# Attention scores' low-key products as two 64-row matmuls, and group copies and query splits moved between VectorE, ScalarE and GpSimd, in a one-core encoder layer

## The chip, the cores and the metric

The kernel runs on one core of one Trainium2 chip. The metric is the device time of one execution in microseconds (us), lower is better. Before the change it was 1474.98 us, the median of three runs (1473.99 to 1475.79).

## The reference

One encoder layer over two sequences, a prompt of 512 tokens and a sample of 1024, with d_model 1024. A normalised input is projected by one matrix to 8 query heads, 2 key heads and 2 value heads of width 64, and to 512 pooling columns. Queries and keys are normalised per head and rotated by position. The part that the change touches is the attention (bidirectional, four query heads for each key head):

```python
s = jnp.einsum('bqkgd,bskd->bkgqs', qi, k, preferred_element_type=jnp.float32) * scale
p = jax.nn.softmax(s, axis=-1).astype(v.dtype)
return jnp.einsum('bkgqs,bskd->bqkgd', p, v)
```

The pooling group, an output projection with residual, and a squared-ReLU MLP (4096 wide) follow. All inputs are float32.

## The kernel before, in words

Float32 operands are split into a rounded high part (type F32R) and a low remainder, and products are summed in PSUM. In the projections and the MLP three products are made of each pair (`three`, L943 to L945: high by high, and the two cross products). The stages are: projection of 12 tiles of 128 tokens, attention of the prompt, attention of the sample, output projection, MLP up and MLP down.

**Attention.** A job is one head's 512 queries against 512 keys for two heads at once (prompt: 4 jobs, called pairs, each with two halves) or one head's 512 queries against 1024 keys (sample: 4 pairs of 4 jobs, `idx` 0 to 3). Each job has 8 steps `k` and 4 score groups `u`. In each step TensorE turns one key tile's probabilities (`transpose_p`, four 128-column transposes, L1088) and multiplies another's with the values (`values`, high and low, L1103 and L1104). In every odd step it also makes the scores of one group of a job that is one or two ahead (`scores`, L1070 and L1072). A group is two 512-column PSUM banks.

**The stacked operands of the scores.** A head is 64 wide and the array has 128 rows. `Qs` holds the high part of the queries on one half of the 128 partitions and the low part on the other. `KA` holds the keys' high part on both halves, `KB` the low part on both. So L1070 makes (q high + q low) by k high and L1072 makes (q high + q low) by k low, each as one matmul of 128 rows by 512 columns for each of the two banks: four in a group.

**Who does what.** ScalarE (ACT) writes `pThi` (rounded, from PSUM), the exponentials `prob` (L1424), the output `o_full`, and the prompt queries' high parts. VectorE (DVE) writes `pTlo` (L1837, PSUM minus `pThi`), the row maxima `nmax` (L1899), reciprocals (L1909), the prompt queries' low parts, and `group_values` (L2022), which gathers half of one key head's values from `V` into `Vg`, twice for each pair of the sample. GpSimd (POOL) makes the sample queries' high and low parts (`split_q`, L2516 and L2519), adds and scales the outputs (L2537, L2543), and computes the pooling windows of the sample (`window_step`). Engines run their own instruction streams in order, written out by hand, and meet at semaphores: a group's scores wait for the exponentials of the group two before (two sets of banks), the `values` matmul waits for `pTlo`, `pTlo` waits for `pThi`, and `pThi` for the transposes. The SP queue moves the other half of each output by DMA (`move_out`) and spreads the reciprocals.

**The end of the projection.** In the last block, VectorE rotates tile 10 (`rotate`, which waits in the middle for a product from GpSimd), and then makes the low values of tile 11 (`split_v`, L1913) and its sum of squares (L1920). TensorE's second score group waits for that `split_v`, since it writes the bank from which it reads. In the same stretch VectorE makes the low queries of pair 1 of the prompt.

Of the kernel before, what the change touches and what calls it, by code (L numbers as in the profile page):

```python
# [7 lines left out]
ALU = mybir.AluOpType  # L8
# [5 lines left out]
P = 128  # L14
# [37 lines left out]
def hybrid_layer(nc, x, g1, w_in, gqk, w_pool, pool_scale, w_out, g2, w_up, w_down,  # L52
                 ident_d, rope_d, edge_d, y):
    with ExitStack() as ctx:
# [3 lines left out]
        def at(name, off, shape, dt=F32):  # L58
            return nc.alloc_sbuf_tensor_at(name, [P] + shape, dt, offset=BASE + off)
# [62 lines left out]
        o_full = at("o_full", S, [2, 512])  # L122
        o_part = at("o_part", S + 4096, [512])
        rinvb = at("rinvb", S + 32768, [512])
        rinvb_last = at("rinvb_last", R + 38912, [512])
        rinvd = nc.dram_tensor("rinvd", [3 * NQ, P, 4], F32).ap()
        sw_sample = [at(f"sw_sample{i}", S + 22528 + i * 4160, [SEQ_S + 2 * PAD]) for i in range(2)]
# [808 lines left out]
        def _(pe):  # L936
# [115 lines left out]
            def scores(s, pair, idx, u):  # L1052
                g = s.group(pair, idx, u)
                half = u // 2 if s.n == 0 else 0
                if u % (GRP // s.halves) == 0:
                    pe.wait_ge(q_lo[s.n], s.out(pair, idx, half) - NQ * s.n + 1)
                pe.wait_ge(k_dup[0], 32 + 32 * s.n)
                if s.n == 0:
                    pe.wait_ge(k_dup[1], 32)

                if not isinstance(g, int) or g >= 2:
                    pe.wait_ge(exp_done, g - 1)
                kv = pair_kv(pair)
                for h in range(2):

                    qt = u if s.n else 2 * (u % 2) + h
                    key0 = h * 512 * s.n
                    out = ps[:, 2 * (u % 2) + h]
                    q = Qs[:, 2 * s.parity(pair, idx) + half, qt * P:(qt + 1) * P]
                    pe.matmul(out, q, KA[s.n][:, bass.ds(kv, 1), key0:key0 + 512].rearrange("p a c -> p (a c)"),  # L1070
                              start=True, stop=False)
                    mm = pe.matmul(out, q, KB[s.n][:, bass.ds(kv, 1), key0:key0 + 512].rearrange("p a c -> p (a c)"),  # L1072
                                   start=False, stop=True)
                mm.then_inc(s_done, 1)

# [107 lines left out]
            scores(seqs[0], 1, 0, 2)  # L1183
            for pair in range(NQ // 2):
                attend(seqs[0], pair)
            with pe.Fori(0, NQ // 2 - 1) as pair:
                attend(seqs[1], pair)
            attend(seqs[1], NQ // 2 - 1, True)

# [142 lines left out]
        def _(act):  # L1332
# [66 lines left out]
            def split_q(s, pair, idx, unit):  # L1399

                j = s.job(pair, idx)
                act.wait_ge(qT_in[s.n], 16 * s.len // P)
                half = s.half_of(idx, unit * s.kts)
                a, c0 = half * 64, s.start + idx // 2 * 512

                if not isinstance(j, int) or j >= 2:
                    act.wait_ge(s_done, GRP * (j - 1))
                if isinstance(j, int) and j == 0 and unit == 0:

                    act.wait_ge(hT_lo, TT)  # L1410
                copy(blocks(Qs[a:a + 64, 2 * s.parity(pair, idx) + unit]), qk_cols(a, pair, c0, 512)).then_inc(q_hi, 1)

            def exps(s, pair, idx, u):
# [79 lines left out]
            def copy_out(s, pair, idx, half):  # L1493
# [5 lines left out]
                    act.wait_ge(o_saved, 2 * n - 3)  # L1499
                copy(o_full[:, half], ps[:, 7]).then_inc(o_copied, 1)  # L1500

            def split_wp():
                act.wait_ge(wp_scaled, 1)
                copy(wphi[:], wpT[:]).then_inc(wp_hi, 1)
# [16 lines left out]
            def attend(s, pair, last=False):  # L1521
                for idx in range(s.per):
                    for k in range(STEPS):
                        if last and (idx, k) == (2, 3):
                            exps(*exped_in(s, pair, idx, k))
                        if last and (idx, k) == (2, 5):
                            split_wp()
                        if transposed_in(s, pair, idx, k):
                            split_p(*transposed_in(s, pair, idx, k))
                        if k % s.kts == s.kts - 1:  # L1530
                            copy_out(s, pair, idx, s.half_of(idx, k))
                        if s.n == 0 and pair == 1 and k == 1:
                            split_q(s, 3, 0, 1)
                        if exped_in(s, pair, idx, k) and not (last and (idx, k) == (2, 3)):
                            exps(*exped_in(s, pair, idx, k))
                        if s.n == 0 and pair == 0 and k == 5:
                            split_q(s, 3, 0, 0)
                        if s.n == 0 and pair == 0 and k == 4:
                            split_q(s, 2, 0, 1)
                        if last and (idx, k) == (2, 6):  # L1540
                            split_c(0)
                        if last and (idx, k) in ((3, 0), (3, 2), (3, 4), (3, 6)):
                            split_folded(k // 2)
# [286 lines left out]
        def _(dve):  # L1830
# [99 lines left out]
                dve.wait_ge(qn_done, FIRST + t + 1)  # L1930
                dve.tensor_tensor(qn[:], qn[:], gqkb[:], ALU.mult).then_inc(qg_done, 1)

            def rotate(t, i):
                dve.wait_ge(qg_done, t + 1)
                dve.wait_ge(rope_in[i % 2], 16 * (t // 2) + 16)

                dve.wait_ge(rT_done, t)
                r = roped[:]
                dve.tensor_tensor(r, qn[:], rope[:, i % 2, 0].unsqueeze(1).to_broadcast([P, NQK, HEAD]),
                                  ALU.mult).then_inc(cos_done, 1)  # L1940
                dve.wait_ge(cos_done, FIRST + t + 1)
                dve.wait_ge(sin_done, FIRST + t + 1)
                dve.tensor_tensor(r, r, qsin[:], ALU.add).then_inc(rope_done, 1)
                dve.wait_ge(rope_done, FIRST + t + 1)
                if t >= 2:
                    dve.wait_ge(rT_out, 64 * (t - 1))
                dve.transpose(rT[t % 2][:], r.rearrange("p (j h) (q c) -> p h q j c", h=2, q=2).rearrange("p h q j c -> p (h q) j c")).then_inc(rT_done, 1)
# [36 lines left out]
            def project_block(n, last):  # L1984
                for i in range(2 if n == 0 else 0, 4):
                    t = n * 4 + i
                    split_v(t, qkv_banks(i) + 1)
                    sum_squares(t)
                    if t + 2 < TT:
                        split_hT(t + 2, (i + 2) % 4)  # L1990
                    if t + 3 < TT:
# [1 line left out]
                    if last and i == 1:  # L1993
# [2 lines left out]
                        split_k(0, 1)  # L1996
                        split_q(0, 0)
                        split_q(0, 1)
                    if last and i == 2:
                        split_q(1, 0)  # L2000
                        split_q(1, 1)
                    if last and i == 3:
                        maxes(seqs[0], 0, 0, 0)
                    scale_qk(t)
                    gain_qk(t)
                    if last and i == 3:
                        maxes(seqs[0], 0, 0, 1)
                    rotate(t, i)
                    if i % 2 and not (last and i == 3):
                        save_u_columns(t // 2)  # L2010

# [1 line left out]
            for n in range(NB - 1):  # L2013
                project_block(n, False)
            project_block(NB - 1, True)

            def group_values(pair, part):

                k0, k1 = part * 4, part * 4 + 4  # L2020
                t0 = SEQS[1][0] // P
                dve.tensor_copy(Vg[:, k0:k1], V[:, t0 + k0:t0 + k1, bass.ds(pair_kv(pair), 1), :]  # L2022
                                .rearrange("p t a d -> p t (a d)").bitcast(F32)).then_inc(vg_done, 1)

            def split_p(s, pair, idx, k):
                dve.wait_ge(pT_hi, s.turn(pair, idx, k) + 1)
# [27 lines left out]
            def attend(s, pair, last=False):  # L2054
                for idx in range(s.per):
                    for k in range(STEPS):
                        if s.n == 0 and pair == 2 and k == 2:
                            group_values(0, 0)
                        if last and (idx, k) == (2, 3):
                            scale_wp()  # L2060
                        if s.n and idx == 3 and k == 6 and not last:

                            dve.wait_ge(pv_done, s.turn(pair, 3, 4))
                            group_values(pair + 1, 0)
                        if transposed_in(s, pair, idx, k):
                            split_p(*transposed_in(s, pair, idx, k))
                        if s.n and (idx, k) == (0, 2):

                            dve.wait_ge(pv_done, s.turn(pair, 0, 0))
                            group_values(pair, 1)  # L2070
                        if inverted_in(s, pair, idx, k):
                            inverses(*inverted_in(s, pair, idx, k))
                        if scored_in(s, pair, idx, k):
# [338 lines left out]
        def _(pool):  # L2412
# [93 lines left out]
            def split_q(s, pair, idx):  # L2506
# [4 lines left out]
                if done:  # L2511
                    pool.wait_ge(win_step, done)
                pool.wait_ge(qT_in[s.n], 16 * s.len // P)
                pool.wait_ge(s_done, GRP * (s.job(pair, idx) - 1))
                pool.wait_ge(q_hi, NQ + m - 1)
                pool.tensor_scalar(blocks(Qs[a:a + 64, 2 * (idx % 2)]), qk_cols(a, pair, c0, 512), 1.0, 1.0, ALU.mult, ALU.mult  # L2516
                                   ).then_inc(q_hi, 1)
                pool.wait_ge(q_hi, NQ + m)
# [43 lines left out]
            def split_k(kv, low, part=0):  # L2562
# [9 lines left out]
                else:  # L2572
# [3 lines left out]
                                       blocks(KA[1][a:a + 64, kv, c].bitcast(F32)), ALU.subtract).then_inc(k_lo, 1)  # L2576
                    pool.wait_ge(k_lo, NKV + kv + part + 1)

            pool.wait_ge(u_saved, FIRST + TT // 2)

            pool.wait_ge(u_done, FIRST + TT // 2)
            window_step(done)
            done += 1
            pool.wait_ge(win_step, done)
            pool.wait_ge(q_hi, 5)
            pool.wait_ge(q_lo[0], 4)
            pool.tensor_tensor(blocks(Qs[64:, 0]), qk_cols(0, 2, 0, SEQ_P), blocks(Qs[0:64, 0].bitcast(F32)), ALU.subtract).then_inc(q_lo[0], 1)
            pool.wait_ge(q_lo[0], 5)
            for s in seqs:
                for pair in range(NQ // 2):  # L2590
                    for idx in range(s.per):
# [163 lines left out]
```

## Time and profile before

| | |
|---|---|
| median of three runs | 1474.98 us |
| the profiled execution's own time | 1475.89 us |
| its span | 1474.1 us |
| TensorE busy | 1463.4 us, 99% of the span |
| VectorE, ScalarE, GpSimd busy | 72%, 49%, 27% |
| mean granted TensorE clock | 0.999 of full speed |

Busy time of TensorE is modelled: the record of a 512-column matmul is about 0.39 us long, and the next one starts 0.23 us after it. What a matmul costs in a stream is therefore read from the starts, not from the length of a record. For the other engines too the records overlap a little at their ends. "Idle before" is the time in which an engine stood still ahead of a record, with the one that released it.

### The profile page before, as it was taken

How to read it: one execution, taken by the hardware profiler on the slowest of the kernel's cores; microseconds unless marked ns; L12 is line 12 of the kernel's file. 1: busy time of each engine (PE TensorE's matmuls, PEld its weight loads, DVE VectorE, ACT ScalarE, POOL GpSimd, SP SyncE). 2: the span in 40 equal slices, each digit the busy share in tenths (PEclk: the TensorE clock that was granted, in tenths of full speed). 3: DMA queues.
4: the chain of work that ended last, by engine and by line, in shares of the span. 5: the costliest groups of instructions: out<-in, count | busy, mean ns of one | idle time of the engine just before them, and what ended most of it. 6: DMA issues, size and time to landing. Idle time of an engine off the chain costs nothing.

```text
span 1474.1 us, 23234 instructions
## 1 busy us (share of the span) xinstructions
PE 1463.4 (99%) x7812; PEld 1306.9 (89%) x7812; DVE 1055.7 (72%) x1254; ACT 729.1 (49%) x1251; POOL 398.1 (27%) x363
## 2 busy tenths in 40 slices
PE   9999999999999999999999999999999999999999
PEld 8999878888888889999999999999888888888887
DVE  6765799999868785544454454449887888878875
ACT  6232398888847755545555554546322322323220
POOL 3457567666745420000000000001220211311300
PEclk9999999999999999999999999999999999999999
DMA  8644341111245849333233334347644344343434
GB/s 263 149 119 118 82 126 34 40 25 24 81 164 192 292 154 380 128 144 141 103 143 133 136 114 151 121 174 278 253 157 158 100 157 126 117 155 109 138 97 183
DMA packets 94443, 212.30 MB, mean 144 GB/s; under 512 B 12080, under 2 KB 31408, under 8 KB 94256
## 3 DMA queue, kind: packets, MB, share of 16 engines
q1 hardware_dynamic: 92192, 200.46, 40.8%
q10 hardware_dynamic: 2192, 11.08, 1.8%
q8 instruction: 33, 0.54, 0.2%
q14 instruction: 26, 0.21, 0.1%
HBM read 133.08 MB, written 71.62 MB: 139 GB/s over the span
## 4 chain that ended last, share of the span: by engine, by line
PE 97%; ACT 1%; DVE 1%; issue 1%; DMA 0%; POOL 0%; ACTq 0%; SPq 0%; DVEq 0%; POOLq 0%
PE ps L943 24%; PE ps L944 24%; PE ps L945 24%; PE ps L1206 6%; PE ps L1088 4%; PE ps L1216 3%; PE ps L1103 2%; PE ps L1070 2%; PE ps L1104 2%; PE ps L1072 2%; ACT prob L1424 0%; DMA ident<-in_ident 0%; ACT pThi L1339 0%; PE ps L968 0%; PE ps L972 0%
## 5 line engine op out<-in xcount | busy, mean ns | idle before, releaser
L943 PE MATMUL ps<-h,wuhi 128*128 128x384 f32 (+1 forms) x904 | 301.5, 333 | 0.2 <-issue 0.2
L944 PE MATMUL ps<-h,wuhi 128*128 128x384 f32 (+1 forms) x904 | 301.1, 333 | 0.0
L945 PE MATMUL ps<-h,wulo 128*128 128x384 f32 (+1 forms) x904 | 301.1, 333 | 0.0
L943 PE MATMUL ps<-wdhi,hidhi 128*128 128x512 f32 x672 | 261.6, 389 | 0.0
L945 PE MATMUL ps<-wdhi,hidlo 128*128 128x512 f32 x672 | 261.5, 389 | 0.0
L944 PE MATMUL ps<-wdlo,hidhi 128*128 128x512 f32 x672 | 261.5, 389 | 0.0
L2328 DVE TENSOR_TENSOR yacc<-yacc,ps 128x1024 f32<-128x1024 f32 x167 | 203.1, 1216 | 78.8 <-PE ps L945 78.8
L1339 ACT ACTIVATE hidhi<-hin 128x1024 fp32r<-128x1024 f32 (+1 forms) x72 | 86.8, 1205 | 301.0 <-PE ps L945 291.8
L2242 DVE TENSOR_TENSOR u<-u,ps 128x384 f32<-128x384 f32 x96 | 53.0, 553 | 181.6 <-PE ps L945 181.6
L943 PEld LDWEIGHTS ps<-h,wuhi 128*128 128x128 f32 x904 | 169.7, 188 | 0.7 <-issue 0.4
L944 PEld LDWEIGHTS ps<-h,wuhi 128*128 128x128 f32 x904 | 169.7, 188 | 0.0
L945 PEld LDWEIGHTS ps<-h,wulo 128*128 128x128 f32 x904 | 169.7, 188 | 0.0
L943 PEld LDWEIGHTS ps<-wdhi,hidhi 128*128 128x128 f32 x672 | 126.1, 188 | 26.8 <-issue 0.4
L944 PEld LDWEIGHTS ps<-wdlo,hidhi 128*128 128x128 f32 x672 | 126.1, 188 | 26.1
L945 PEld LDWEIGHTS ps<-wdhi,hidlo 128*128 128x128 f32 x672 | 126.1, 188 | 26.1
L2684 POOL TENSOR_TENSOR hout<-h,hout 128x384 f32<-128x384 f32 x1 | 1.7, 1748 | 477.3 <-PE ps L945 477.3
L1837 DVE TENSOR_TENSOR pTlo<-ps,pThi 128x512 fp32r<-128x512 f32 x160 | 107.9, 686 | 12.4 <-ACT pThi L1339 9.6
L1837 DVE TENSOR_TENSOR hidlo<-hin,hidhi 128x1024 fp32r<-128x1024 f32 (+1 forms) x72 | 111.5, 1549 | 5.4 <-ACT hidhi L1339 5.4
L1643 ACT ACTIVATE hout<-u 128x384 f32<-128x384 f32 x96 | 50.4, 525 | 124.8 <-DVE u L2242 113.5
L1339 ACT ACTIVATE pThi<-ps 128x512 fp32r<-128x512 f32 x160 | 95.0, 601 | 26.4 <-PE ps L1088 19.7
L1088 PEld LDWEIGHTS ps<-ident,prob 128*128 128x128 f32 x640 | 79.3, 140 | 22.7 <-DVE pTlo L1837 1.4
L1424 ACT ACTIVATE prob<-ps,nmax 128x1024 f32<-128x1024 f32 (+1 forms) x96 | 93.0, 974 | 11.5 <-DVE nmax L1899 11.3
(229 smaller groups left out, 2813.8 us busy)
## 6 DMA issues: line engine op xcount, KB each, us to landing
hd<-hout SPq DMA_DIRECT2D x64, 384.0 KB, 3.2
hin<-hd SPq DMA_DIRECT2D x48, 512.0 KB, 3.6
hd<-hout SPq DMA_DIRECT2D x32, 576.0 KB, 2.8
hin<-hd SPq DMA_DIRECT2D x24, 768.0 KB, 4.4
wuraw<-in_w_up SPq DMA_DIRECT2D x17, 1024.0 KB, 5.9
wdraw<-in_w_down SPq DMA_DIRECT2D x8, 2048.0 KB, 9.3
h<-h2d ACTq DMA_DIRECT2D x7, 1536.0 KB, 10.8
x2in<-in_x SPq DMA_DIRECT2D x12, 512.0 KB, 3.3
```

The lines of the kernel that those rows point to most:

```text
L943: pe.matmul(out, w_hi, m_hi, start=start, stop=False, skip_group_check=resumed)
L944: pe.matmul(out, w_hi, m_lo, start=False, stop=False, skip_group_check=resumed)
L945: return pe.matmul(out, w_lo, m_hi, start=False, stop=stop, skip_group_check=resumed)
L1088: mm = pe.transpose(ps[:, 4 + k % 3, qt * P:(qt + 1) * P], prob[s.parity(pair, idx)][:, u, c0:c0 + P], ident[:])
L1206: pe.matmul(ps[:, 2 * i + h], c[i][:, k], wohi[:, j, h * 512:(h + 1) * 512], start=(j == 0 and c is chi), stop=False)
L1216: mm = pe.matmul(ps[:, 2 * i + h], chi[i][:, SLOT_ROWS[j]], wolo[:, j, h * 512:(h + 1) * 512], start=False, stop=(n == KT - 1))
L1339: return act.activation(out, in_, ACT.Copy, **kw)
L1424: ins = act.activation(prob[b][:, u, c0:c0 + s.len], psw[:, (u % 2) * 1024 + c0:(u % 2) * 1024 + c0 + s.len], ACT.Exp, bias=nmax[:, b, q:q ...
L1643: act.activation(out, src, ACT.Relu).then_inc(relu_done, 1)
L1837: return dve.tensor_tensor(out, a, b.bitcast(F32), ALU.subtract)
L2242: dve.tensor_tensor(u, u, up_bank(par, (1, 4, 5)[k]), ALU.add).then_inc(u_sum, 1)
L2328: dve.tensor_tensor(q, q, down_banks(u, o), ALU.add).then_inc(acc_done, 1)
```

## The change

1. **Scores.** In `scores`, the two L1070 products come first, then the two with `KB`. For the prompt's pairs 0 and 1 these keep all 128 rows. For the prompt's pairs 2 and 3 and all of the sample each uses 64 rows: bank 0 is made from partitions 0 to 63 and bank 1 from 64 to 127, both with the high queries. (The product of the two low parts is left out there.) A new tile `Qh` holds the high queries on the half where `Qs` has the low ones. TensorE's loop over the sample's first three pairs is written out.
2. **Filling Qh.** ScalarE copies it for prompt pairs 2 and 3 (four copies of 64x512, behind a wait for the last pooling projection), GpSimd for the sample (one for each job).
3. **`group_values`** goes from VectorE to ScalarE, at the same steps.
4. **Low queries of prompt pair 1** go from VectorE's tile 10 to GpSimd, behind its product for tile 11's rotation.
5. **Tile 11's `split_v` and sum of squares** go into the middle of `rotate` of tile 10.

```diff
+        Qh = at("Qh", S + 34816, [2, 512], F32R)
...
                 for h in range(2):
-
-                    qt = u if s.n else 2 * (u % 2) + h
-                    key0 = h * 512 * s.n
-                    out = ps[:, 2 * (u % 2) + h]
-                    q = Qs[:, 2 * s.parity(pair, idx) + half, qt * P:(qt + 1) * P]
-                    pe.matmul(out, q, KA[s.n][:, bass.ds(kv, 1), key0:key0 + 512].rearrange("p a c -> p (a c)"),
+                    c, keys, out = part(h)
+                    pe.matmul(out, Qs[:, 2 * slot + half, c], KA[s.n][:, bass.ds(kv, 1), keys].rearrange("p a c -> p (a c)"),
                               start=True, stop=False)
-                    mm = pe.matmul(out, q, KB[s.n][:, bass.ds(kv, 1), key0:key0 + 512].rearrange("p a c -> p (a c)"),
+                for h in range(2):
+                    c, keys, out = part(h)
+                    if s.n == 0 and pair < 2:
+                        r = slice(0, P)
+                    else:
+                        r = slice(h * 64, h * 64 + 64)
+                    q = Qh[r, slot, c] if r.stop - r.start == 64 and h != high else Qs[r, 2 * slot + half, c]
+                    mm = pe.matmul(out, q, KB[s.n][r, bass.ds(kv, 1), keys].rearrange("p a c -> p (a c)"),
                                    start=False, stop=True)
...
-            with pe.Fori(0, NQ // 2 - 1) as pair:
+            for pair in range(NQ // 2 - 1):
...
+                if s.n == 0 and pair >= 2:
+                    act.wait_ge(u_done, FIRST + TT // 2)
+                    copy(blocks(Qh[64 - a:128 - a, s.parity(pair, idx)]), qk_cols(a, pair, c0, 512))
...
+            def group_values(pair, part):
+
+                k0, k1 = part * 4, part * 4 + 4
+                t0 = SEQS[1][0] // P
+                copy(Vg[:, k0:k1], V[:, t0 + k0:t0 + k1, bass.ds(pair_kv(pair), 1), :]
+                     .rearrange("p t a d -> p t (a d)").bitcast(F32)).then_inc(vg_done, 1)
...
+                        if s.n == 0 and pair == 2 and k == 2:
+                            act.wait_ge(v_lo, FIRST + TT)
+                            group_values(0, 0)
+                        if s.n and idx == 3 and k == 6 and not last:
+
+                            act.wait_ge(pv_done, s.turn(pair, 3, 4))
+                            group_values(pair + 1, 0)
+                        if s.n and (idx, k) == (0, 2):
+
+                            act.wait_ge(pv_done, s.turn(pair, 0, 0))
+                            group_values(pair, 1)
...
+                between()
                 dve.wait_ge(cos_done, FIRST + t + 1)
...
-                    if last and i == 2:
-                        split_q(1, 0)
-                        split_q(1, 1)
...
+                    if last and i == 2:
+                        def last_values():
+                            split_v(t + 1, qkv_banks(i + 1) + 1)
+                            sum_squares(t + 1)
+                        rotate(t, i, last_values)
...
+                pool.tensor_scalar(blocks(Qh[b:b + 64, idx % 2]), qk_cols(a, pair, c0, 512), 1.0, 1.0, ALU.mult, ALU.mult)
                 pool.tensor_scalar(blocks(Qs[a:a + 64, 2 * (idx % 2)]), qk_cols(a, pair, c0, 512), 1.0, 1.0, ALU.mult, ALU.mult
...
+            def split_prompt_q(pair, unit):
+
+                a, b, m = unit * 64, (1 - unit) * 64, 2 * pair + unit
+                slot = 2 * (pair % 2) + unit
+                pool.wait_ge(q_hi, m + 1)
+                pool.wait_ge(q_lo[0], m)
+                pool.tensor_tensor(blocks(Qs[b:b + 64, slot]), qk_cols(a, pair, 0, SEQ_P),
+                                   blocks(Qs[a:a + 64, slot].bitcast(F32)), ALU.subtract).then_inc(q_lo[0], 1)
+                pool.wait_ge(q_lo[0], m + 1)
+
+            pool.wait_ge(sin_done, FIRST + TT)
+            split_prompt_q(1, 0)
+            split_prompt_q(1, 1)
...
-            pool.wait_ge(q_hi, 5)
-            pool.wait_ge(q_lo[0], 4)
-            pool.tensor_tensor(blocks(Qs[64:, 0]), qk_cols(0, 2, 0, SEQ_P), blocks(Qs[0:64, 0].bitcast(F32)), ALU.subtract).then_inc(q_lo[0], 1)
-            pool.wait_ge(q_lo[0], 5)
+            split_prompt_q(2, 0)
```

## Rows read from the trace of the kernel before

**Rows 1.** The page: TensorE's busy time, and the ending chain by engine.

```profile
PE 1463.4 (99%) x7812; PEld 1306.9 (89%) x7812; DVE 1055.7 (72%) x1254; ACT 729.1 (49%) x1251; POOL 398.1 (27%) x363
...
PE 97%; ACT 1%; DVE 1%; issue 1%; DMA 0%; POOL 0%; ACTq 0%; SPq 0%; DVEq 0%; POOLq 0%
```

**Rows 2.** Stretches of the attention: busy time of each engine in each.

```profile
core 0: us, PE busy (x) PEld busy (x) DVE busy (x) ACT busy (x) POOL busy (x), PEclk, DMA share, GB/s
257.00:267.92 10.92, 10.92 (x66) 9.16 (x65) 10.16 (x14) 9.61 (x18) 7.83 (x9) 1.00 0.33 72
...
190.00:215.00 25.00, 24.05 (x133) 18.81 (x133) 23.37 (x33) 23.73 (x59) 15.99 (x14) 1.00 0.41 118
...
240.00:360.00 120.00, 120.00 (x707) 100.74 (x705) 113.24 (x149) 105.58 (x188) 81.09 (x65) 1.00 0.13 29
```

**Rows 3.** TensorE's timeline around one score group: start, length, line.

```profile
262.23 0.40 PE L1072 MATMUL ps<-KB,Qs 128*128 x1
262.47 0.39 PE L1070 MATMUL ps<-KA,Qs 128*128 x1
262.70 0.40 PE L1072 MATMUL ps<-KB,Qs 128*128 x1
262.93 0.39 PE L1103 MATMUL ps<-pThi,Vg 128*128 128x512 f32 x1
```

**Rows 4.** The weight loads of the same stretch.

```profile
261.89 0.19 PEld L1070 LDWEIGHTS ps<-KA,Qs 128*128 128x128 f32 x1
262.00 0.19 PEld L1072 LDWEIGHTS ps<-KB,Qs 128*128 128x128 f32 x1
262.24 0.19 PEld L1070 LDWEIGHTS ps<-KA,Qs 128*128 128x128 f32 x1
```

**Rows 5.** VectorE's groups in four sample jobs, 257 to 300.68 us.

```profile
L1837 DVE TENSOR_TENSOR pTlo<-ps,pThi 128x512 fp32r<-128x512 f32 x33 | 22.3, 687 | 2.1 <-ACT pThi L1339 1.4
L1899 DVE TENSOR_REDUCE nmax<-ps 128x1 f32<-128x1024 f32 x16 | 19.4, 1215 | 0.3
L2022 DVE CAST Vg<-V 128x512 fp32r x2 | 1.4, 694 | 0.0
```

**Rows 6.** ScalarE's and GpSimd's groups in the same four jobs.

```profile
L1339 ACT ACTIVATE pThi<-ps 128x512 fp32r<-128x512 f32 x33 | 19.7, 598 | 5.5 <-PE ps L1088 3.9
...
L2519 POOL TENSOR_TENSOR Qs<-QT,Qs 64x512 fp32r<-64x512 f32 x4 | 5.1, 1283 | 0.3
L2516 POOL TENSOR_SCALAR Qs<-QT 64x512 fp32r<-64x512 f32 x4 | 2.5, 629 | 0.4
```

**Rows 7.** The end of the projection, in order of time.

```profile
169.07 0.74 ACT L1442 ACTIVATE qksq<-qk 128x640 f32<-128x640 f32 x1
...
171.15 0.83 DVE L1943 TENSOR_TENSOR roped<-roped,qsin 128x640 f32<-128x640 f32 x1 [1.67 <-POOL qsin L2485]
...
172.78 0.31 DVE L1913 SCALAR_TENSOR_TENSOR V<-ps,rs,V 128x128 fp32r<-128x128 f32 x1
...
173.19 0.47 PE L1070 MATMUL ps<-KA,Qs 128*128 128x512 f32 x1 [1.31 <-issue]
```

**Rows 8.** The copy of values at 365 us and who works beside it.

```profile
365.10 2.39 POOL L2468 TENSOR_TENSOR up<-sw_sample,up 128x1024 f32<-128x1024 f32 x1
...
365.46 2.32 DVE L2022 CAST Vg<-V 128x512 fp32r x1
...
368.52 0.47 PE L1103 MATMUL ps<-pThi,Vg 128*128 128x512 f32 x1 [0.92 <-DVE pTlo L1837]
```

**Rows 9.** ScalarE's prompt outputs (one each half job) and a query copy.

```profile
194.61 0.59 ACT L1339 ACTIVATE o_full<-ps 128x512 f32<-128x512 f32 x1
...
213.19 0.59 ACT L1339 ACTIVATE o_full<-ps 128x512 f32<-128x512 f32 x1
...
235.42 0.59 ACT L1339 ACTIVATE o_full<-ps 128x512 f32<-128x512 f32 x1
...
185.88 0.63 ACT L1339 ACTIVATE Qs<-QT 64x512 fp32r<-64x512 f32 x1
187.34 0.69 ACT L1424 ACTIVATE prob<-ps,nmax 128x512 f32<-128x512 f32 x1 [0.83 <-DVE nmax L1899]
```

More of the change, by code:

```diff
@@ L1063, in scores, with part @@
                 kv = pair_kv(pair)
-                for h in range(2):
-                    qt = u if s.n else 2 * (u % 2) + h
-                    key0 = h * 512 * s.n
-                    out = ps[:, 2 * (u % 2) + h]
-                    q = Qs[:, 2 * s.parity(pair, idx) + half, qt * P:(qt + 1) * P]
-                    pe.matmul(out, q, KA[s.n][:, bass.ds(kv, 1), key0:key0 + 512].rearrange("p a c -> p (a c)"),
-                              start=True, stop=False)
-                    mm = pe.matmul(out, q, KB[s.n][:, bass.ds(kv, 1), key0:key0 + 512].rearrange("p a c -> p (a c)"),
+                slot = s.parity(pair, idx)
+                high = idx % 2 if s.n else half
+                def part(h):
+                    qt = u if s.n else 2 * (u % 2) + h
+                    return slice(qt * P, (qt + 1) * P), slice(h * 512 * s.n, h * 512 * s.n + 512), ps[:, 2 * (u % 2) + h]
+                for h in range(2):
+                    c, keys, out = part(h)
+                    pe.matmul(out, Qs[:, 2 * slot + half, c], KA[s.n][:, bass.ds(kv, 1), keys].rearrange("p a c -> p (a c)"),
+                              start=True, stop=False)
+                for h in range(2):
[6 more added lines that the diff above has]
+                    mm = pe.matmul(out, q, KB[s.n][r, bass.ds(kv, 1), keys].rearrange("p a c -> p (a c)"),
                                    start=False, stop=True)
@@ L1931, in gain_qk, with rotate @@
                 dve.tensor_tensor(qn[:], qn[:], gqkb[:], ALU.mult).then_inc(qg_done, 1)
-            def rotate(t, i):
+            def rotate(t, i, between=lambda: None):
                 dve.wait_ge(qg_done, t + 1)
@@ L1986, in project_block @@
                     t = n * 4 + i
-                    split_v(t, qkv_banks(i) + 1)
-                    sum_squares(t)
+                    if not (last and i == 3):
+                        split_v(t, qkv_banks(i) + 1)
+                        sum_squares(t)
                     if t + 2 < TT:
@@ L2007, in project_block @@
                         maxes(seqs[0], 0, 0, 1)
-                    rotate(t, i)
+                    if last and i == 2:
[3 more added lines that the diff above has]
+                        rotate(t, i, last_values)
+                    else:
+                        rotate(t, i)
                     if i % 2 and not (last and i == 3):
@@ L2015, in _ @@
             project_block(NB - 1, True)
[L2017 to L2023, printed above, removed]
             def split_p(s, pair, idx, k):
@@ L2056, in attend @@
                     for k in range(STEPS):
-                        if s.n == 0 and pair == 2 and k == 2:
-                            group_values(0, 0)
                         if last and (idx, k) == (2, 3):
                             scale_wp()
-                        if s.n and idx == 3 and k == 6 and not last:
-                            dve.wait_ge(pv_done, s.turn(pair, 3, 4))
-                            group_values(pair + 1, 0)
                         if transposed_in(s, pair, idx, k):
                             split_p(*transposed_in(s, pair, idx, k))
-                        if s.n and (idx, k) == (0, 2):
-                            dve.wait_ge(pv_done, s.turn(pair, 0, 0))
-                            group_values(pair, 1)
                         if inverted_in(s, pair, idx, k):
```

## The prediction

> **What bounds the kernel now.** I read the page first, then the stretches of the attention, then the timelines inside it. TensorE is busy 99% of the span and makes 97% of the chain that ended last [rows 1]: time leaves this kernel where TensorE gets shorter or waits less, provided that no neighbour takes over. Inside the sample's attention it never stands still: 120.00 of 120 us, and one job takes 10.92 us, while VectorE has 10.16 and ScalarE 9.61 us of records in it [rows 2]. So the neighbours are close behind, and how close decides what a shorter TensorE is worth. The prompt's attention differs: in 25 us TensorE has 24.05, ScalarE 23.73 and VectorE 23.37 us [rows 2], and a half job there took (213.19 - 194.61) / 3 = 6.19 us at first and (235.42 - 213.19) / 4 = 5.56 us later [rows 9], against the 10.92 / 2 = 5.46 us that TensorE's own work takes. There ScalarE sets the pace.
>
> **The score products.** Matmuls of 512 columns start 0.23 us apart [rows 3], so a group's four cost 0.93 us. If the two 64-row products run at the same time, the group has three such slots and saves 0.23 us. Prompt pairs 2 and 3 have 8 groups and the sample 64. Scores are made ahead: job 0 of the prompt makes three of them, each later job four, so 15 are made during the prompt and 57 during the sample, in 57 / 4 = 14.25 jobs. At full worth these 57 give 57 x 0.23 = 13.1 us.
>
> Do the neighbours follow? TensorE's job would be 10.92 - 4 x 0.23 = 10.0 us. VectorE, in four jobs of 43.68 us, stood idle 2.1 + 0.3 us and spent 1.4 us in the copies that now leave it [rows 5]: (43.68 - 2.4 - 1.4) / 4 = 9.97 us of a job. ScalarE stood idle 5.5 us [rows 6] and takes over the two copies, at about 0.6 us each like its own 128x512 copy `pThi` (598 ns): (43.68 - 5.5 + 1.2) / 4 = 9.85 us. Three engines within 0.15 us of one another, in fixed orders with handoffs between them, will not reach the longest of the three. I add 0.15 us a job: 10.15 us. The saving is 14.25 x (10.92 - 10.15) = **11.0 us**.
>
> What the trace of before cannot show is two matmuls side by side, since it has none. The bounds come from the nearest rows. Below: they start together, 0.23 us saved. 
>
> The Trainium skill speaks against this change on that point: "TensorEngine Tiling (Array Packing)", section Tiling Modes, Key Properties, says that changing the tiling mode, not just the tile, drains TensorE. No row of this kernel shows such a change. By that rule the case "above" would hold. The same skill's "TensorE: Matmul & The Clock Gate", Part 3, gives packed tiles a start some 4 ns apart; by that figure alone the 57 groups would give an estimated 57 x 0.226 = 12.9 us.
>
> **Filling Qh.** In the sample GpSimd gets one more copy for each job, 0.63 us [rows 6], on top of 7.83 us in 10.92 [rows 2]. The low queries queued behind it are due only in the next job's fourth step, so it costs nothing; if that cover were gone it would be 0.7 us a job. In the prompt ScalarE gets four copies at 0.63 us [rows 9]. The first stands before the exponentials of pair 1, where ScalarE waited 0.83 us for a maximum [rows 9]; that covers it. The other three fall between 195 and 213 us, where ScalarE sets the pace: **+1.8 us** with what is queued behind them, at the least 0. That the first copy now waits for the last pooling projection costs nothing, since the exponentials just ahead of it ended later than that.
>
> **The rest of the prompt.** From 213.19 us on, two jobs took 22.23 us. With TensorE at 10.0, the exponentials of 1024 columns taking over from pairs of 512, and one `group_values` (0.6) on ScalarE in the first of them, I put these at 10.75 and 10.1 us: **-1.4 us**.
>
> **The values of tile 11.** TensorE stood still 1.31 us before its second score group, which needs the `split_v` that VectorE began at 172.78 and ended 0.1 us before that group's start [rows 7]. VectorE itself had waited 1.67 us for GpSimd inside `rotate`, and ScalarE had finished `qksq` at 169.81 [rows 7]. Both moved operations (0.31 and 0.8 us) fit into that wait, so the whole idle time goes: **-1.3 us**. Next late would be the third group, which needs the first exponentials; these move up too, by some 0.9 us, since the two operations no longer stand before their maxima. The sum of squares also starts GpSimd's chain for tile 11 earlier, by some 2.5 us, which makes room there for the two low-query splits of pair 1 (1.28 us each, as L2519 [rows 6]) before the next group of scores. They cost nothing; if GpSimd were late, up to 2.6 us.
>
> **The copy at 365 us.** VectorE's `group_values` usually takes 0.69 us [rows 5], but this one took 2.32, ending with GpSimd's 2.39-us subtraction beside it, and TensorE then stood still 0.92 us [rows 8]. ScalarE does it now: **-0.9 us**. The other copies were hidden.
>
> Writing out TensorE's loop moves nothing that I can price: the loop's ends showed no idle TensorE [rows 2]. Taking the splits of pair 1 away from VectorE only fills a wait for GpSimd.
>
> **The sum.** -11.0 + 1.8 - 1.4 - 1.3 - 0.9 = -12.8 us. The profiled execution took 1475.9 us (span 1474.1 and 1.8 around it), so one like it would take 1463.1; the median was 0.9 below it, so **1462.2 us** is the forecast.
>
> **Rivals.**
> - *The loads take turns.* The second half product starts 0.11 us after the first. 57 x 0.12 = 6.8 us in place of 11.0, TensorE again alone as the bound: 1466.4 us. For it: loads never start closer than 0.11 us. Against it: they start well ahead of need.
> - *A neighbour becomes the bound.* Handoffs cost 0.5 us a job, not 0.15: the job is 10.5 us, saving 14.25 x 0.42 = 6 us: 1467.2 us. For it: VectorE's 9.97 us is as long as TensorE's.
> - *Nothing runs side by side.* The half products take a slot each. Then only -1.3, -0.9, -0.3 and +1.8 remain: about 1474.3 us.
> - *Slower: the array runs empty at each change of rows.* 72 groups x (0.32 - 0.23) = +6.5 us, with -0.7 from the other edits: about 1480.8 us. It decides against the change as soon as a change of rows costs over (0.23 + 0.01) / 2 = 0.12 us.
>
> **How the numbers follow.** Forecast 0.45, loads in turn 0.17, neighbour 0.14, nothing side by side 0.09, running empty 0.15. About 0.2% (3 us) is what a measurement of this kernel can tell from no change. The first three are faster, and part of the cases between: 0.77; within 0.2%: 0.09; slower: 0.14. The range starts where all 57 groups give 13.1 us and the prompt's copies hide (-16.7 us against the profiled execution, 1458.3) and reaches to the case of nothing side by side, 1474.5. The likeliest case's own range is 1459 to 1465.
>
> **What would show it.** In the changed trace the two `KB` products start within some 0.02 us, and the next matmul 0.23 us later; a sample job takes 10.0 to 10.3 us, with TensorE waiting now and then for `pTlo` or `prob`; the idle 1.31 and 0.92 us are gone; the prompt's first half jobs are longer than 6.19 us. The forecast is wrong if the second `KB` product, or the matmul after it, starts later than that, or if VectorE shows no idle time while TensorE does.

## The result: slower, and the profile after

The changed kernel takes 1484.55 us (median of six runs, 1483.89 to 1485.83) against 1474.8 for the kernel before (median of its six): a ratio of 1.0070, with a 95% interval of 1.0060 to 1.0081. That is 9.75 us slower where 12.8 us faster was forecast. The profiled execution took 1484.44 us with a span of 1482.6.

The page of the profile says first where the time is. TensorE is still the bound, and its busy time grew by 9.6 us over that of [rows 1], although it has the same number of instructions:

```profile
PE 1473.0 (99%) x7812; PEld 1286.2 (87%) x7812; DVE 1054.7 (71%) x1244; ACT 734.7 (50%) x1263; POOL 409.3 (28%) x381
...
PE 96%; ACT 1%; DVE 1%; issue 1%; DMA 0%; POOL 0%; ACTq 0%; SPq 0%; DVEq 0%; POOLq 0%
```

The stretch inside the sample's attention, as in [rows 2]. The second row is one job, now 11.58 us long instead of 10.92:

```profile
core 0: us, PE busy (x) PEld busy (x) DVE busy (x) ACT busy (x) POOL busy (x), PEclk, DMA share, GB/s
240.00:360.00 120.00, 120.00 (x669) 84.00 (x667) 106.24 (x137) 101.59 (x182) 83.60 (x74) 1.00 0.14 28
...
270.75:282.33 11.58, 11.58 (x67) 8.13 (x66) 10.18 (x14) 9.94 (x19) 7.77 (x7) 1.00 0.13 23
```

TensorE never waits there, and in 120 us it starts 669 matmuls where it started 707. VectorE is busy 106.24 us and not 113.24: it has become idler, so it is not the bound. What TensorE does with its time is seen in its timeline around a group (start, length, line; L1099 are the transposes, L1074 the products with `KA`, L1083 those with `KB`, L1114 and L1115 the values), to be read against [rows 3]:

```profile
243.33 0.60 PE L1099 MATMUL ps<-ident,prob 128*128 128x128 f32 x4
243.69 0.71 PE L1074 MATMUL ps<-KA,Qs 128*128 128x512 f32 x2
244.33 0.49 PE L1083 MATMUL ps<-KB,Qs 64*128 64x512 f32 x1
244.33 0.49 PE L1083 MATMUL ps<-KB,Qh 64*128 64x512 f32 x1
244.75 0.50 PE L1114 MATMUL ps<-pThi,Vg 128*128 128x512 f32 x1
245.09 0.39 PE L1115 MATMUL ps<-pTlo,Vg 128*128 128x512 f32 x1
245.32 0.60 PE L1099 MATMUL ps<-ident,prob 128*128 128x128 f32 x4
```

The same group of the kernel before [rows 3] lies between these two sets of transposes, 1.83 us apart:

```profile
261.56 0.60 PE L1088 MATMUL ps<-ident,prob 128*128 128x128 f32 x4
...
263.39 0.60 PE L1088 MATMUL ps<-ident,prob 128*128 128x128 f32 x4
```

The two 64-row products do start together, at 244.33. But they start 0.64 us after the first product with `KA`, where two such slots took 0.55 us before (in its trace from 261.92 to 262.47). The next matmul starts 0.42 us after them, not 0.23, and the one after that another 0.34 us later. The weight loads of the same stretch, as in [rows 4], show what stands in between:

```profile
243.66 0.30 PEld L1074 LDWEIGHTS ps<-KA,Qs 128*128 128x128 f32 x2
244.33 0.18 PEld L1083 LDWEIGHTS ps<-KB,Qs 64*128 64x128 f32 x1 [0.36 <-issue]
244.33 0.18 PEld L1083 LDWEIGHTS ps<-KB,Qh 64*128 64x128 f32 x1
244.75 0.19 PEld L1114 LDWEIGHTS ps<-pThi,Vg 128*128 128x128 f32 x1 [0.24 <-issue]
244.86 0.19 PEld L1115 LDWEIGHTS ps<-pTlo,Vg 128*128 128x128 f32 x1
```

In [rows 4] a load begins while the matmul ahead of it runs, and costs nothing. Here the 64-row loads begin only 0.36 us after the last load ended, and the first 128-row load after them 0.24 us after those. The group "weight loads of L1083, waiting for nothing that the profile shows" has 42 such gaps of up to 0.4 us in 120 us, one for each group:

```profile
PEld ps L1083 <- issue: 15.2, 42, 0.4
```

VectorE's idle time in four jobs (270.75 to 316.9 us), where [rows 5] had 2.1 us, and the copies of values on ScalarE, 0.62 us each (four jobs are 46.15 us long here, so one is 11.54):

```profile
L1869 DVE TENSOR_TENSOR pTlo<-ps,pThi 128x512 fp32r<-128x512 f32 x33 | 22.8, 691 | 5.4 <-ACT pThi L1350 4.7
...
L1350 ACT ACTIVATE Vg<-V 128x512 fp32r x2 | 1.2, 622 | 0.0
```

The prompt's outputs, as in [rows 9]: the first is 2.4 us earlier than before, the fourth 0.4 us earlier, the last 0.4 us later. (The first is as early, at 192.56, in the run with the 64-row products alone, which has none of the moves; so those 2.4 us can't be put down to them.)

```profile
192.17 0.59 ACT L1350 ACTIVATE o_full<-ps 128x512 f32<-128x512 f32 x1
...
212.80 0.59 ACT L1350 ACTIVATE o_full<-ps 128x512 f32<-128x512 f32 x1
...
235.84 0.59 ACT L1350 ACTIVATE o_full<-ps 128x512 f32<-128x512 f32 x1
```

From there to the end of the span the changed kernel needs 1482.6 - 235.84 = 1246.8 us and the one before 1474.1 - 235.42 = 1238.7: 8.1 us, nearly all of the difference in span. The last output of the sample's attention shows that 7.8 of them lie in it: 419.79 - 235.84 = 183.95 us against 411.61 - 235.42 = 176.19.

```profile
411.61 0.60 ACT L1339 ACTIVATE o_full<-ps 128x512 f32<-128x512 f32 x1 [0.42 <-PE ps L1104]
...
419.79 0.60 ACT L1350 ACTIVATE o_full<-ps 128x512 f32<-128x512 f32 x1 [0.44 <-PE ps L1115]
```

### The profile page after: what moved, and what is told of

Its sections match the earlier page's. It is cut to its first block, busy times and chain, and to the rows that moved or that the text cites. A ratio compares the mean times of both kernels' runs of the same rounds, so it can differ in the third digit from the quotient of the medians.

```text
span 1482.6 us, 23091 instructions
## 1 busy us (share of the span) xinstructions
PE 1473.0 (99%) x7812; PEld 1286.2 (87%) x7812; DVE 1054.7 (71%) x1244; ACT 734.7 (50%) x1263; POOL 409.3 (28%) x381
## 4 chain that ended last, share of the span: by engine, by line
PE 96%; ACT 1%; DVE 1%; issue 1%; DMA 0%; POOL 0%; ACTq 0%; SPq 0%; DVEq 0%; POOLq 0%
PE ps L944 24%; PE ps L945 24%; PE ps L946 24%; PE ps L1217 6%; PE ps L1099 4%; PE ps L1114 3%; PE ps L1227 3%; PE ps L1115 2%; PE ps L1074 2%; PE ps L1083 2%; ACT prob L1438 0%; DMA ident<-in_ident 0%; ACT pThi L1350 0%; PE ps L969 0%; PE ps L978 0%
## 5 line engine op out<-in xcount | busy, mean ns | idle before, releaser
L1099 PEld LDWEIGHTS ps<-ident,prob 128*128 128x128 f32 x640 | 77.5, 140 | 25.7 <-issue 5.7
L1931 DVE TENSOR_REDUCE nmax<-ps 128x1 f32<-128x1024 f32 (+1 forms) x80 | 97.3, 1217 | 1.1 <-PE ps L1083 0.5
```

The source lines that it names most:

```text
L1099: mm = pe.transpose(ps[:, 4 + k % 3, qt * P:(qt + 1) * P], prob[s.parity(pair, idx)][:, u, c0:c0 + P], ident[:])
L1931: dve.tensor_reduce(nmax[:, s.parity(pair, idx), u * s.tiles:(u + 1) * s.tiles], psw[:, (u % 2) * 1024:(u % 2) * 1024 + 1024].rearrange("p ...
```

## The experiments

The rivals were that the moved edits or the loop cost the time (B), that two products at once are slow in themselves (C), or that a 64-row pair is slow wherever it stands (D). All ratios below are to the kernel before, run beside them (medians 1474.14, 1474.48 and 1474.41 us in the three sets; 1474.8 beside the changed kernel). A difference between runs of two sets is therefore good to some tenths.

**All 128 rows, all else as changed.**

```diff
-                    if s.n == 0 and pair < 2:
-                        r = slice(0, P)
-                    else:
-                        r = slice(h * 64, h * 64 + 64)
+                    r = slice(0, P)
```

> The changed kernel, but every product with KB uses all 128 rows (Qh is still written and not read). Theory A (each change between 128 and 64 rows makes TensorE finish first and load weights in the open; the changed trace shows 1.99 us from one set of transposes over a group to the next where the kernel before shows 1.83, so 0.16 us for each of 72 groups): 1484.5 - 11.5 = about 1473 us, 1.8 us below before. Theory B (the moved edits, ScalarE's and GpSimd's extra copies or the written-out loop cost the time, and the side-by-side products are even or better): stays near 1484.

Measured: 1474.69 us, ratio 1.0006 (0.9997 to 1.0015). 9.9 us of the changed kernel's time go with this one line, so B falls. It is 1.7 us above what I expected; the runs further down put this down to the copies into `Qh`. In its trace the sample's attention takes 410.32 - 235.29 = 175.03 us, 8.9 less than in the changed kernel: 0.16 us for each of 57 groups. Its timeline has the same group, with loads hidden: four products in 1.01 us and no gap behind them.

```profile
242.69 0.71 PE L1074 MATMUL ps<-KA,Qs 128*128 128x512 f32 x2
243.24 0.62 PE L1080 MATMUL ps<-KB,Qs 128*128 128x512 f32 x2
243.70 0.40 PE L1111 MATMUL ps<-pThi,Vg 128*128 128x512 f32 x1
243.93 0.39 PE L1112 MATMUL ps<-pTlo,Vg 128*128 128x512 f32 x1
244.16 0.60 PE L1096 MATMUL ps<-ident,prob 128*128 128x128 f32 x4
```

From the first product with `KA` to the next transposes these are 1.47 us, against 1.63 in the changed kernel: the 0.16 us again.

**The 64-row products alone**, on the kernel before: `scores`, the copies into `Qh` and the written-out loop as in the change, the rest as before.

> The kernel before with only the 64-row products, the Qh copies that they need and the written-out loop; group_values, the low queries of pair 1 and tile 11's values stay where they were. Theory A: 1474.8 + 11.5 + up to 1.8 for the copies in the prompt = 1486 to 1488 us. Theory B: at or below 1477, since what costs the time is not in it.

Measured: 1487.14 us, ratio 1.0092 (1.0077 to 1.0107). Within the range of A. It is 2.6 us above the changed kernel, of which the moves (alone, below) are 1.5; its four executions lie 3.2 us apart, so the rest says little.

**One half only.** Bank 0's product uses 64 rows and bank 1's all 128 (which adds bank 1's product of the two low parts again).

```diff
-                    if s.n == 0 and pair < 2:
+                    if (s.n == 0 and pair < 2) or h:
```

> The changed kernel, but only bank 0's product with KB uses 64 rows, bank 1's uses all 128: the same two changes of rows in a group, and nothing at the same time. Theory A: four slots of 0.23 us and the 0.40 us of two changes, so 0.24 us more than the changed kernel for each of 72 groups, 17 us: about 1501 us. Rival C (the cost comes from two products that run at once, in the array or in their PSUM banks): no such cost here, so a group costs 0.93 us and the time is about 1473.

Measured: 1501.70 us, ratio 1.0187 (1.0172 to 1.0203), as A has it: 17.2 us above the changed kernel, 0.24 us a group. So C falls: with nothing at the same time the two changes cost as much as before, and the slot that the pair had saved is lost too. In its trace the group takes 2.22 us, and both loads stand in the open again:

```profile
242.96 0.60 PE L1099 MATMUL ps<-ident,prob 128*128 128x128 f32 x4
...
245.18 0.60 PE L1099 MATMUL ps<-ident,prob 128*128 128x128 f32 x4
...
243.96 0.18 PEld L1083 LDWEIGHTS ps<-KB,Qs 64*128 64x128 f32 x1 [0.36 <-issue]
244.38 0.19 PEld L1083 LDWEIGHTS ps<-KB,Qs 128*128 128x128 f32 x1 [0.24 <-issue]
```

**Each pair twice** (the low-key product is counted twice).

```diff
+                for turn in range(2 if s.n or pair >= 2 else 1):
...
-                                   start=False, stop=True)
+                                   start=False, stop=turn == (1 if s.n or pair >= 2 else 0))
```

> The changed kernel with the two 64-row products with KB issued twice in a row in each of the 72 groups, into the same banks (so the low-key product is counted twice). Theory A (the cost sits in the change of rows, not in the products): the second pair adds one slot of 0.23 us, or 0.34 if two 64-row loads can't be hidden under a 64-row product: +17 to +24 us on 1484.5, 1501 to 1509. Rival D (a pair of 64-row products takes about 0.42 us wherever it stands, as from its start to the next matmul in the changed trace): +30 us, 1515.

Measured: 1502.02 us, ratio 1.0187 (1.0171 to 1.0203): 17.5 us above the changed kernel, 72 x 0.243. D falls: a second pair costs one slot, like any matmul of 512 columns. Its timeline and its loads show the difference between entering and staying:

```profile
244.22 0.49 PE L1084 MATMUL ps<-KB,Qs 64*128 64x512 f32 x1
244.22 0.49 PE L1084 MATMUL ps<-KB,Qh 64*128 64x512 f32 x1
244.55 0.39 PE L1084 MATMUL ps<-KB,Qs 64*128 64x512 f32 x1
244.56 0.39 PE L1084 MATMUL ps<-KB,Qh 64*128 64x512 f32 x1
244.88 0.50 PE L1115 MATMUL ps<-pThi,Vg 128*128 128x512 f32 x1
...
244.32 0.19 PEld L1084 LDWEIGHTS ps<-KB,Qs 64*128 64x128 f32 x1
244.33 0.19 PEld L1084 LDWEIGHTS ps<-KB,Qh 64*128 64x128 f32 x1
244.88 0.19 PEld L1115 LDWEIGHTS ps<-pThi,Vg 128*128 128x128 f32 x1 [0.37 <-issue]
```

The second pair's loads begin at 244.32, while the first pair runs; only the load that returns to 128 rows waits, until 244.88. This trace also takes the price apart. The first pair has its load in the open and no change behind it, and the next start comes after 0.33 us; the second has its loads hidden and a change behind it, and the next start comes after 0.33 us again (244.55 to 244.88). So about 0.10 us of a change lies ahead of the new load and 0.10 us is the load itself in the open.

**The pair ahead of the products with KA.**

```diff
+                if tiled:
+                    with_low(True)
+                    mm = with_high(False)
```

> The changed kernel with the 64-row pair ahead of the two products with KA, so that the first change of rows comes behind transposes (128 columns) or a values product and the second ahead of KA. Theory A with a wait for the last matmul to finish and an open load at each change: the same two changes, 1484.5 within 2 us if both costs are fixed; up to 8 us less (0.11 us a group) if the exposed load behind the transposes, which is there anyway (the second matmul after them starts 0.31 us later and not 0.23), is shared. If the order mattered for another reason (bank 0 begun by a 64-row product), it would be slower than 1487.

Measured: 1486.94 us, ratio 1.0087 (1.0071 to 1.0102), 2.4 us above the changed kernel. Nothing was shared with the exposed load behind the transposes: a group takes 2.01 us (243.56 to 245.57 in its trace), so moving the two changes to another place in the group gains nothing. The 2.4 us are 0.4 more than I had allowed for equal costs. The 0.02 us a group make 72 x 0.02 = 1.4 of them; where the rest comes from is open.

**Four changes in a group.** KA and KB of bank 0, then KA and KB of bank 1.

> The changed kernel with the products in the old order, KA and KB of bank 0, then KA and KB of bank 1, the KB products still on 64 rows: four changes of rows in a group and nothing side by side. Theory A: four slots and two times 0.40 us, 0.63 us a group more than the changed kernel, 72 x 0.63 = 45 us: about 1530. Rival C (the cost is in running two at once): 1473 to 1480.

Measured: 1526.78 us, ratio 1.0355 (1.0339 to 1.0370): 42.2 us above the changed kernel, 0.59 us a group, where A had 0.63 and C nothing. Here every matmul shown stands between two changes:

```profile
245.49 0.50 PE L1081 MATMUL ps<-KB,Qh 64*128 64x512 f32 x1
245.92 0.50 PE L1074 MATMUL ps<-KA,Qs 128*128 128x512 f32 x1
246.35 0.49 PE L1081 MATMUL ps<-KB,Qs 64*128 64x512 f32 x1
246.78 0.50 PE L1112 MATMUL ps<-pThi,Vg 128*128 128x512 f32 x1
```

Starts are 0.43 us apart instead of 0.23: **0.20 us for each change of rows**. Each of these intervals holds one open load and one wait ahead of the next load, behind 64 rows and behind 128 alike.

**The moves alone**: `group_values` on ScalarE, the low queries of pair 1 on GpSimd, tile 11's values in the rotation; `scores`, loop and queries as before.

> The kernel before with only the moves: group_values on ScalarE, low queries of pair 1 on GpSimd, tile 11's values in the rotation's wait; scores, loop and queries as before, no Qh copies. Theory A: the two idle times of 1.31 and 0.92 us go and nothing is added: 1472 to 1473 us, faster than both kernels. Theory B (the moves load ScalarE where it sets the pace): 1475 or more.

Measured: 1472.63 us, ratio 0.9989 (0.9980 to 0.9998). It is faster than both kernels, if only by 1.5 us against the one before. The profiled execution of this kernel was its slowest (1476.21 us; the ten others took 1472.1 to 1473.4) and has one wait of 2.5 us in the MLP, far from the change.

**The moves with ScalarE's copies.** The expectation speaks of both engines' copies, but this kernel had only ScalarE's four; GpSimd's were missing.

> The kernel with the moves alone (1472.6), plus the copies into Qh on ScalarE and GpSimd, which nobody reads; the scores stay on 128 rows and the loop stays a loop. If the three copies on ScalarE in the prompt, where it sets the pace, are what separates the moves alone from the changed kernel with all rows: +1.8 to +2.1 us, 1474.4 to 1474.7. If the written-out loop or the order of the four products is: 1472.6.

Measured: 1476.47 us, ratio 1.0012 (1.0003 to 1.0021), 3.8 us above the moves alone. Expected were 1.8 to 2.1. Two rows of its trace, of VectorE and GpSimd, and TensorE's longest wait for the probabilities' low part (in all, times, longest) show where most of the difference stands:

```profile
210.02 2.39 DVE L1859 TENSOR_TENSOR Qs<-QT,Qs 64x512 fp32r<-64x512 f32 x1
...
209.86 2.00 POOL L2477 TENSOR_TENSOR up<-sw_sample,up 128x1024 f32<-128x1024 f32 x1
...
PE ps L1089 <- DVE pTlo L1859: 2.4, 2, 1.8
```

**The moves with all copies**, the kernel that was meant:

> The moves alone with all of the copies into Qh, ScalarE's in the prompt and GpSimd's in the sample. (The run called e9_moves_and_copies had only ScalarE's four: in its trace GpSimd, with no copy ahead, began its subtraction at 209.86 us, just before VectorE's query split at 210.02, which then took 2.39 us instead of 0.95.) Theory: which of the two begins first decides; with GpSimd's copy ahead VectorE's split begins first again, and the time is 1474.4 to 1474.7, as with all rows in the changed kernel. Rival: the copies themselves cost the 3.8 us, and it stays at 1476.5 or goes higher.

Measured: 1475.55 us, ratio 1.0006 (0.9997 to 1.0015). The time lies between the two that I had written down, 0.9 us above the upper end of the theory's and as much below the rival's. In the trace the order is back: VectorE's split takes 0.94 us, and TensorE waits 0.38 us (at 211.89) where it waited 1.84 (at 213.19).

```profile
210.18 0.94 DVE L1859 TENSOR_TENSOR Qs<-QT,Qs 64x512 fp32r<-64x512 f32 x1
...
210.66 2.32 POOL L2477 TENSOR_TENSOR up<-sw_sample,up 128x1024 f32<-128x1024 f32 x1
```

**The moves with the loop written out.**

> The moves alone, with TensorE's loop over three pairs of the sample written out. Expected: 1472.6, no difference from the loop, as the loop's ends show no idle TensorE. Rival: 1 us or more either way.

Measured: 1472.86 us, ratio 0.9993 (0.9984 to 1.0002), 0.2 us from the loop: no difference.

**Tile 11's values alone.**

> The kernel before with only tile 11's low values and sum of squares moved into the wait of tile 10's rotation. Expected: the idle time ahead of TensorE's second score group goes; it was 1.31 us in the profiled execution of before but 0.19 in that of the kernel with the 64-row products alone, so 0.2 to 1.3 us faster than before: 1473.0 to 1474.1.

Measured: 1473.61 us, ratio 0.9995 (0.9986 to 1.0004). The median is 0.8 us lower, inside what was expected, but the interval does not exclude no change. The idle time is gone in its trace: the second score group starts 3.79 us after the first (168.05 and 171.84 us), as in the changed kernel, where it was 5.26 us (167.93 to 173.19) in the profiled execution of before.

**group_values alone.**

> The kernel before with only group_values on ScalarE. Expected: the 0.92 us at 365 us go, the copy in the prompt costs at most 0.5: 1473.3 to 1474.0. Rival: it makes no difference, since VectorE's copies were all hidden but for a chance meeting: 1474.3.

Measured: 1473.80 us, ratio 0.9996 (0.9987 to 1.0005), 0.6 us lower, again inside the interval of no change. In its trace the outputs around the old stall are 375.02 - 364.21 = 10.81 us apart, against 378.37 - 366.37 = 12.00 in the one of before. The stall itself was no accident of one execution: both other kernels that still have the copy on VectorE show it in their traces, the one with the 64-row products alone (2.51 us, at 373.12) and the one with tile 11's values alone:

```profile
364.04 2.30 DVE L2030 CAST Vg<-V 128x512 fp32r x1
```

## Why the prediction was wrong, point by point

**What bounds the kernel** held: TensorE before and after, with VectorE within 0.03 us a job of it by the prediction's own numbers (10.0 and 9.97), had the slot been saved. That closeness was never tested, because TensorE's job grew to 11.5 us.

With 0.20 the rival's sum would have been 72 x (0.40 - 0.24) - 0.7 = +10.8, 1485.8 us, 1.2 above what was measured. The gap is about what the prompt hides, where ScalarE sets the pace: its 15 groups would cost 15 x 0.16 = 2.4 us, but from its first output to its last the changed kernel takes 43.67 us and the one with all 128 rows 42.77, 0.9 more. The Trainium skill's rule, in "TensorEngine Tiling (Array Packing)", section Key Properties, that a change of tiling mode drains TensorE and a change of tile does not, agrees with these traces: 0.20 us for a change, and between the two pairs of the run with each pair twice only the 0.10 us of the first pair's own load. That the new load is held back by a drain is what the Trainium skill says; the records show only how long it is held back. I had weighed it against hidden loads that all stayed in one mode, which say nothing about it; a rule that speaks against a change wanted a larger share than 0.15.

**Loads in turn** fell: both halves' loads begin at the same time (244.33). **A neighbour as the bound** wasn't reached.

**Filling Qh**: in the prompt +1.8 us was forecast. From the first to the fourth output the changed kernel takes 20.63 us and the one before 18.58: +2.05. The copies alone account for it: with all 128 rows it is 20.65, with the moves and all copies 20.63, with the moves alone 18.58. In time the copies are worth 2.1 us (all 128 rows against moves alone) to 2.7 us (moves with all copies against the moves with the loop written out, beside it). With GpSimd's copies added to ScalarE's the time fell by 0.9 us, so they cost nothing on balance.

**The rest of the prompt** was to give -1.4 us, from TensorE's shorter groups and ScalarE. Those groups are longer now, and the four half jobs took 23.04 us against 22.23: +0.8, which is the rows again, since with all 128 rows they took 22.12.

**The values of tile 11** went as described, but the 1.31 us were those of one execution. In the kernel with the 64-row products alone, where the edit is not in, TensorE waited only 0.19 us at that place, and with `group_values` alone 0.21. The median gained 0.8 us, within an interval that includes no gain. **The copy at 365 us**: the stall is gone, 1.2 us between outputs in the trace, 0.6 us in the median, where the interval again includes no gain. (That a copy "usually takes 0.69 us" was the mean of two of 0.41 and 0.97 us.) The low queries of pair 1 were never moved alone; the moves together give 1.5 us and these two 0.8 + 0.6, so nothing is left over for them. **Writing out the loop**: nothing, as said.

Together: moves -1.5, copies +2.1, rows +9.9, a sum of +10.5 us against +9.75 measured. This is no independent check: each term is the step from one kernel to the next on the way to the changed one, so the gap only shows how far medians of different sets lie apart. A second way, the 64-row products with their copies alone (+13.0) and the moves (-1.5), gives +11.5, 1.7 us above what was measured. The account is good to that much and no better; why the two ways differ is open.

## What to carry to other kernels

In this kernel products on half the rows side by side save one slot for each pair, 0.24 us for 512 columns, and pay 0.20 us each time TensorE goes from one row count to the other. With one pair between two changes that is a loss of 0.16 us. By an estimate from the same numbers two pairs in a row would win 2 x 0.24 - 0.40 = 0.08 us, and only longer runs on half the rows would win much; no run here had them. Before splitting a matmul into halves, count the changes in the stream, not the matmuls. Loads that cost nothing in the trace of before did so in the order of that trace: ask what lets them start early, and whether the new instruction keeps that.

## What the runs showed of the hardware

A change between 128-row and 64-row matmuls costs 0.20 us (starts 0.43 us apart instead of 0.23), about 0.10 ahead of the new load and 0.10 for the load. Behind transposes it was no cheaper than behind products of 512 columns (pair first, 2.01 us a group against 1.99). Two 64-row products with different rows and banks start within 0.01 us, and their two loads as well. Between 128-row matmuls, loads do begin under the running one: a load of 128 rows starts at 262.24, under a matmul of 128 rows that started at 262.23 ([rows 3] and [rows 4]). The Trainium skill's "TensorE: Matmul & The Clock Gate", Part 3, The mechanism, says two things on that: its text lets a load go ahead of matmuls in flight where the row group does not conflict or where it goes to the background weight buffer, and its list says that the two overlap only when the row group differs. The list does not hold for these traces.

Which of VectorE and GpSimd begins first decides a collision. VectorE's split, which reads two operands from SBUF, took 0.94 us when it began 0.48 us ahead of GpSimd's subtraction, and 2.39 us when it began 0.16 us behind it; GpSimd's took 2.32 us in the first case and 2.00 in the second. The stall at 365 us [rows 8] has the same form. The Trainium skill's "SBUF — State Buffer", section SBUF: two separate sides, describes it as an exclusive lock on a shared port pair that whoever starts first holds for the whole instruction. The numbers agree in who waits. They agree only roughly in how long: the split ended 0.55 us behind GpSimd's record and the copy at 365 us 0.29 us behind it, less than the 0.94 us and the 0.41 us or more that they take elsewhere, and GpSimd's records are rough. Leaving out a copy of 0.6 us on GpSimd, which nobody waited for, so made the kernel 0.9 us slower in the median (1476.47 against 1475.55, each beside its own runs of the kernel before, 1474.48 and 1474.41).
